# Two weight sums moved to the DMA queues, and two of seven block products with a 512-column operand

## The reference

```python
h = h + 0.5 * swiglu(rms_norm(h, norms[i, 0]), ffn_w_gate[i, 0], ffn_w_up[i, 0], ffn_w_down[i, 0])
...
h = h + 0.5 * swiglu(rms_norm(h, norms[i, 2]), ffn_w_gate[i, 1], ffn_w_up[i, 1], ffn_w_down[i, 1])
```

## Time and profile before

| | |
|---|---|
| median of 3 runs | 1891.37 us (1891.32 to 1891.40) |
| the profiled execution, its own time | 1889.01 us |
| its span, first to last instruction | 1887.2 us |
| TensorE busy | 1858.4 us, 98% |
| VectorE, ScalarE, GpSimd busy | 1354.8, 895.7, 260.9 us |
| stage with the 18 tiles of f = 1 | 521.8 to 703.9 us from the start |
| moved by DMA | 179.88 MB, mean 95 GB/s |

### The profile page before, as it was taken

How to read it: one execution, slowest core, us unless ns; L and a number is a source line. 1 busy time by engine, 2 the same in 40 slices (tenths; PEclk the granted TensorE clock), 3 DMA queues, 4 the chain that set the end, 5 groups by cost and what they waited for, 6 DMA issues and landing times.

```text
span 1887.2 us, 31448 instructions
## 1 busy us (share of the span) xinstructions
PE 1858.4 (98%) x11418; PEld 1615.1 (86%) x11418; DVE 1354.8 (72%) x1983; ACT 895.7 (47%) x1509; POOL 260.9 (14%) x204
## 2 busy tenths in 40 slices
PE   8999999999999999999999999999989999999998
PEld 6899988777799998887899998877658899998886
DVE  8788788774988874357888864269984988874355
ACT  7455542245555563234455553244563655554222
POOL 0000001312100000234000001073243100000225
PEclk9999999999999999999999999999999999999999
DMA  5233333332233333323333332232101233333321
GB/s 180 90 112 101 99 106 105 96 100 86 78 98 95 109 112 111 111 67 101 100 92 99 111 123 96 93 109 68 57 1 46 91 100 99 111 105 118 105 74 56
DMA packets 56753, 179.88 MB, mean 95 GB/s; under 512 B 12144, under 2 KB 12144, under 8 KB 56656
## 3 DMA queue, kind: packets, MB, share of 16 engines
q1 hardware_dynamic: 54656, 173.69, 29.7%
q0 software_dynamic: 928, 3.02, 0.5%
q10 hardware_dynamic: 1088, 2.10, 0.3%
HBM read 175.04 MB, written 3.15 MB: 94 GB/s over the span
## 4 chain that ended last, share of the span: by engine, by line
PE 87%; DVE 9%; ACT 2%; POOL 1%; issue 1%; DMA 0%; DVEq 0%; SPq 0%; POOLq 0%; ACTq 0%
PE ps L2314 36%; PE ps L2276 26%; PE ps L2258 17%; PE ps L2762 2%; PE ps L2425 1%; DVE work L1256 1%; DVE sm L1280 1%; DVE stat L1254 1%; POOL sumsq L1556 1%; DVE x_lo L441 1%; ACT prob L1998 0%; PE ps L2476 0%; PE ps L2288 0%; DVE sm L1299 0%; PE ps L2711 0%
## 5 line engine op out<-in xcount | busy, mean ns | idle before, releaser
L389 DVE TENSOR_TENSOR w_lo<-raw,w_hi 128x1024 fp32r<-128x1024 f32 x174 | 231.6, 1340 | 217.0 <-ACT w_hi L381 216.3
L381 ACT ACTIVATE w_hi<-raw 128x1024 fp32r<-128x1024 f32 x186 | 194.2, 1054 | 293.9 <-PE ps L2276 248.7
L2314 PE MATMUL ps<-xs_hi,w_hi 128*128 128x256 f32 x1088 | 308.2, 283 | 0.5
L2314 PE MATMUL ps<-xs_lo,w_hi 128*128 128x256 f32 x1088 | 307.9, 283 | 0.0
L2314 PE MATMUL ps<-xs_hi,w_lo 128*128 128x256 f32 x1088 | 307.9, 283 | 0.0
L2276 PE MATMUL ps<-act_hi,w_hi 128*128 (+1 forms) x720 | 280.5, 390 | 0.0
L2276 PE MATMUL ps<-act_lo,w_hi 128*128 (+1 forms) x720 | 280.1, 389 | 0.0
L2276 PE MATMUL ps<-act_hi,w_lo 128*128 (+1 forms) x720 | 280.1, 389 | 0.0
L2258 PE MATMUL ps<-x_hi,w_hi 128*128 128x512 f32 x640 | 257.5, 402 | 8.5 <-ACT w_hi L381 7.2
L2258 PE MATMUL ps<-x_hi,w_lo 128*128 128x512 f32 x640 | 250.2, 391 | 0.0
L2258 PE MATMUL ps<-x_lo,w_hi 128*128 128x512 f32 x640 | 249.8, 390 | 0.0
(11 more groups left out here) (412 smaller groups left out, 3545.5 us busy)
## 6 DMA issues: line engine op xcount, KB each, us to landing
raw<-in_weights SPq DMA_DIRECT2D x322, 512.0 KB, 3.6
h<-in_xT ACTq DMA_DIRECT2D x4, 512.0 KB, 6.4
out<-result SPq DMA_DIRECT2D x4, 512.0 KB, 3.0
p_raw<-in_pT POOLq DMA_DIRECT2D x2, 512.0 KB, 4.2
scratch_u<-u_sc SPq DMA_DIRECT2D x1, 512.0 KB, 6.6
u_grp<-scratch_u SPq DMA_DIRECT2D x1, 512.0 KB, 4.1
scratch_y<-y_grp SPq DMA_DIRECT2D x2, 256.0 KB, 3.1
y_ch<-scratch_y SPq DMA_DIRECT2D x1, 512.0 KB, 3.6
```

Source lines behind the costliest of these rows:

```text
L381: act.activation(w_hi[:, slot], raw[:, slot], ACT.Copy).then_inc(hi_ready, 1)
L389: dve.tensor_tensor(w_lo[:, slot], raw[:, slot], w_hi[:, slot].bitcast(F32), SUB)\
L2314: last = pe.matmul(ps[:, bank, 0:HALF], w[:, at, cols], x[:, k], start=(start and k == 0 and part == 0), stop=(stop and k == KH - 1 and pa ...
```

## The change

1. **Sums 1 and 2.** VectorE's 1024-column addition goes. ScalarE's queue loads gate block halves into w_sum[0] and up block halves into w_sum[1], two DMAs of 256 KB; GpSimd waits for them and issues two DMAs that add the left half of the up chunk to both. Odd tiles use a second buffer, `other_sums`, over the first two tiles of act_hi. The loads are issued three tiles ahead (`load_ahead`), at the end of a tile ahead of `silu_right`, after a wait for the last remainder of the tile whose buffer is used again; those of the first two tiles lie in the passage ahead of the first SiLU.
2. **Products B21 and T4.** x_hi and x_lo become the two halves of one tensor, `x_parts`. A product of these two is now, per k-step, one matmul of w_hi by both parts, 512 columns, and one of w_lo by x_hi, 256 columns. The two halves of the bank have to be added afterwards: `gate_left` becomes two additions, and for the right gate half ScalarE copies the bank's right half out, VectorE adds the left half (`gate_right`), and SiLU follows in place.
3. **Order.** In a common tile T2 and T4 are split one by one (512 columns each), T4 first, and the product of gate and up of a tile moves into the next tile, behind its sums. ScalarE's loop ends one turn earlier, as the last tiles load nothing ahead.

```diff
+        x_parts, at_x = sb("x_parts", [P, 2, KD, T], F32R)
+        x_hi, x_lo = x_parts[:, 0], x_parts[:, 1]
...
+        other_sums = over("other_sums", [P, 2, T], at_hi)
...
 def weight_sums(i, b):
-                dve.tensor_tensor(w_sum[:, 0:2], own[:, 0:4:3],
-                                  own[:, 2].unsqueeze(1).to_broadcast([P, 2, T]), ADD)\
-                   .then_inc(fast["w_sums"], 1)
+                dve.wait_ge(added(b), turns_of(f, i, b))
+                dve.tensor_tensor(w_sum[:, 2], loaded_sums(b)[:, 0], own[:, 3], ADD)\
                    .then_inc(fast["w_sums"], 1)
...
 def gate_left(i, b):
+                dve.tensor_tensor(t1[:, b % 2, 0:HALF], left[:, 0:HALF],
+                                  part_sum[:, 0, HALF:], ADD).then_inc(fast["folded"], 1)
+                dve.wait_ge(fast["folded"], counted(1, f, i, b, 1))
+                dve.tensor_tensor(t1[:, b % 2, 0:HALF], left[:, HALF:], t1[:, b % 2, 0:HALF],
+                                  ADD).then_inc(s["gate_scaled"], 1)
+            def gate_right(i, b):
+                dve.wait_ge(fast["half_copied"], counted(1, f, i, b, 1))
+                dve.tensor_tensor(t1[:, b % 2, HALF:], ps[:, banks_of(b)[0], 0:HALF],
+                                  t1[:, b % 2, HALF:], ADD).then_inc(fast["right_scaled"], 1)
...
 def fast_tile(i, b):                                   # VectorE
+                dve.wait_ge(fast["t_ready"], counted(2, f, i, b, 2))
                 weight_sums(i, b + 1)
-                sums_lo(i, b + 1, 0)
+                product(i, b - 1)
+                fourth_lo(i, b + 1)
+                second_lo(i, b + 1)
                 gate_left(i, b)
                 own_lo(i, b + 1, 0)
                 up_right(i, b)
                 sums_lo(i, b + 1, 1)
                 own_lo(i, b + 1, 1)
                 up_left(i, b)
-                product(i, b)
+                gate_right(i, b)
...
+        def block_sums(pool, f, first):                # GpSimd
+            def sums(i, b):
+                pool.wait_ge(loaded(b), turns_of(f, i, b))
+                pool.dma_start(dst[:, 0], up[:, 0:T], accum_op=ADD).then_inc(added(b), 16)
+                pool.dma_start(dst[:, 1], up[:, 0:T], accum_op=ADD).then_inc(added(b), 16)
...
+            def load_blocks(i, b):                     # ScalarE
+                act.dma_start(dst[:, 0], gate[:, 0:T]).then_inc(loaded(b), 16)
+                act.dma_start(dst[:, 1], up[:, T:]).then_inc(loaded(b), 16)
+
+            def load_ahead(i, b):
+                act.wait_ge(fast["t_ready"], counted(2, f, i, b - 2, 2))
+                act.wait_ge(fast["w_sums"], counted(2, f, i, b - 2, 1))
+                load_blocks(i, b)
...
 def silu_right(i, b):
-                act.activation(t1[:, b % 2, HALF:], ps[:, banks_of(b)[0], 0:HALF], ACT.Silu)\
+                act.activation(t1[:, b % 2, HALF:], ps[:, banks_of(b)[0], HALF:], ACT.Copy)\
+                   .then_inc(fast["half_copied"], 1)
+                act.wait_ge(fast["right_scaled"], counted(1, f, i, b, 1))
+                act.activation(t1[:, b % 2, HALF:], t1[:, b % 2, HALF:], ACT.Silu)\
                    .then_inc(s["silu_done"], 1)
...
+            def fast_tile(i, b, ahead=True):           # ScalarE
                 copy_part(i, b, 0)
                 copy_part(i, b, 1)
                 copy_part(i, b, 2)
-                sums_hi(i, b + 1, 0)
+                fourth_hi(i, b + 1)
+                second_hi(i, b + 1)
                 own_hi(i, b + 1, 0)
                 copy_part(i, b, 3)
                 sums_hi(i, b + 1, 1)
                 silu_left(i, b)
                 own_hi(i, b + 1, 1)
+                if ahead:
+                    load_ahead(i, b + 3)
                 silu_right(i, b)
...
+            def paired(bank, at, both, start, stop, done):     # TensorE
+                for k in range(KH):
+                    pe.matmul(ps[:, bank], wf_hi[:, at, k * P:(k + 1) * P], both[:, :, k],
+                              start=(start and k == 0), stop=False, skip_group_check=True)
+                for k in range(KH):
+                    last = pe.matmul(ps[:, bank, 0:HALF], wf_lo[:, at, k * P:(k + 1) * P],
+                                     both[:, 0, k], start=False, stop=(stop and k == KH - 1),
+                                     skip_group_check=True)
+                last.then_inc(done, 1)
...
-                product(left_bank, at["B21"], *unmixed(5), True, True, fast["product"])
+                paired(left_bank, at["B21"], both(5), True, True, fast["product"])
...
-                product(first_bank, at["T4"], *unmixed(6), False, True, chunk_used)
+                paired(first_bank, at["T4"], both(6), False, True, chunk_used)
```

More of the change, by code:

```diff
@@ L1558, in sum_squares @@
                 pool.wait_ge(sum_step, done)
+        def block_sums(pool, f, first):
+            plain = PLAINS[f]
+            pair = plain // 2
+            def sums(i, b):
+                dst = loaded_sums(b)
+                up = A["weights"][bass.ds(i * 4 + (first + 2 * b + 1), 1)]\
+                    .rearrange("a p b f -> (a p) (b f)")
+                pool.wait_ge(loaded(b), turns_of(f, i, b))
+                pool.dma_start(dst[:, 0], up[:, 0:T], accum_op=ADD).then_inc(added(b), 16)
+                pool.dma_start(dst[:, 1], up[:, 0:T], accum_op=ADD).then_inc(added(b), 16)
+            sums(pair, 0)
+            sums(pair, 1)
+            with pool.Fori(pair + 1, NF // 2, 1) as i:
+                sums(i, 0)
+                sums(i, 1)
         def s5_loads(pool):
@@ L1652, in _ @@
             sum_squares(pool, 4)
+            block_sums(pool, 2, STARTS[5])
             sum_squares(pool, 5)
@@ L1728, in gained @@
                        .then_inc(fast["x_gained"], 1)
+            def load_blocks(i, b):
+                gate, up = (A["weights"][bass.ds(i * 4 + (first + 2 * b + k), 1)]
+                            .rearrange("a p b f -> (a p) (b f)") for k in range(2))
+                dst = loaded_sums(b)
+                act.dma_start(dst[:, 0], gate[:, 0:T]).then_inc(loaded(b), 16)
[4 more added lines that the diff above has]
+                load_blocks(i, b)
             def own_hi(i, b, which):
@@ L1784, in opening_tile @@
             def opening_tile():
+                load_ahead(pair, 2)
                 copy_part(pair, 0, 0)
@@ L1794, in opening_tile @@
                 own_hi(pair, 1, 1)
+                load_ahead(pair, 3)
                 silu_right(pair, 0)
-            def fast_tile(i, b):
+            def fast_tile(i, b, ahead=True):
                 copy_part(i, b, 0)
@@ L1841, in passage_of_six @@
                     gained(range(KD))
+                load_blocks(pair, 0)
+                load_blocks(pair, 1)
                 silu(0)
@@ L1897, in ffn_up_act @@
             fast_tile(pair, 1)
-            with act.Fori(pair + 1, NF // 2 - 1, 1) as i:
+            with act.Fori(pair + 1, NF // 2 - 2, 1) as i:
                 fast_tile(i, 0)
                 fast_tile(i, 1)
-            fast_tile(NF // 2 - 1, 0)
+            fast_tile(NF // 2 - 2, 0)
+            fast_tile(NF // 2 - 2, 1, ahead=False)
+            fast_tile(NF // 2 - 1, 0, ahead=False)
             last_tile(NF // 2 - 1, 1)
```

64 lines of the change are left out of this document (51 added, 13 removed).

## The result

The changed kernel takes 1970.58 us (median of 4 runs, 1969.30 to 1975.82) against 1891.38: a ratio of 1.0424, 95% interval 1.0405 to 1.0443. The forecast was 1898.0, with a range that ended at 1914. The loss of 79 us is what the third rival described, at a chance of 0.08.

The account below looks back on a forecast made before the run. The prediction took TensorE's own stream, busy 98% of the span, as the bound. It summed -7.2 + 7.0 + 4.8 + 2.0 = +6.6 us on 1889.0, plus 2.4 for the median: 1898.0 us, range 1886 to 1914.

Parts of the forecast that it names:

- Rival 3: GpSimd's adding DMAs land late: beyond 7.2 us a tile grows by half the excess; at 9 us about 1948; chance 0.08.
- The transfers: Loads and adding DMAs for the sums land at 20.5 us, before VectorE's sum needs them at 21.8: cost 0.
- cover: Time the transfers may slip before a tile suffers, 2.7 us; beyond it half of each microsecond late falls on a tile.
- ScalarE's round: In 44 loop tiles ScalarE's issues and closing copy make product 3 0.16 us late: tiles of 10.13 us, 7.0 us in all.
- X: Delay on ScalarE from the T1/T3 remainder's end to the closing copy, for two DMA issues: 1.17 us; under 1.01 costs nothing.
- Last tiles: Last tile of each stage: two act_high operations ahead of the first copy make product 3 0.49 us late, 2.0 in all.
- Openings: Second tile of each stage: load_ahead waits for the T2/T4 remainder, product 3 is 1.2 us late, four times, 4.8.
- First load_ahead: The load_ahead before the first copy costs nothing: its two issues fit beside ScalarE's work.
- The gain: Products B21 and T4 on TensorE: 544 fewer matmuls at 0.0133 us each, 7.2 us less, a tile of 9.97 us.
- Rival 1: Not slower: ScalarE's round of waits stays under TensorE's, X below 1.01; 1884.2 to 1891.0 us; chance 0.30.
- Rival 2: ScalarE's DMA issue costs 0.487 us: +21.5, 1912.9 us; chance 0.14.
- Rival 4: A wide matmul over two separate halves takes its pair's time: +13.8 us without the 7.2 gain; chance 0.02.

Follow-up runs that it names:

- e4: The changed kernel with GpSimd's second DMAs plain, overwriting instead of adding: 1911.4 us, ratio 1.0107.
- e1: The changed kernel without GpSimd's adding DMAs, VectorE's first sum and ScalarE's T1/T3 split waiting for the plain loads instead: 1905.0 us, ratio 1.0076.
- e5: The changed kernel without GpSimd's adding DMAs and with the loops of ScalarE, VectorE and GpSimd written out, addresses constant: 1891.8 us, ratio 1.0008.
- e7: The changed kernel with four buffers for the sums, loads issued two tiles earlier, and loops of ScalarE, VectorE and GpSimd written out: 1896.0 us, ratio 1.0027.

## Why the prediction was wrong, and where it was right

**The step that failed is "The transfers": cost 0, cover 2.7 us.** It took the load's landing from raw's median, 3.6 us, and the adding DMA's from the latest plain one, 4.5, calling neither a bound. Measured in the chain: 7.09 and 7.35 (medians of the second of each pair: 6.5 and 7.3). By the forecast's own account, from the first issue to the sum, 3.6 + 1.3 + 4.5 = 9.4 us; measured 659.07 - 642.92 = 16.2. The 6.7 us more are 2.7 of cover and 4.0 late, half per tile: 2.0, a tile of 12.0. It is 11.6 in this round (11.4 on the mean), because the part of the ring outside the transfers shrank too: the forecast had 9.2 us from VectorE's sum (offset 1.9) to the issue (11.1), the chain has 642.92 - 635.93 = 7.0. That part contained waits for TensorE, which close up once TensorE is no longer the slowest.

Three facts were wrong in it. The adding was priced as a copy, and it holds the DMA engines 2.15 times as long. Plain, the second DMA of a pair lands after a median of 3.4 us (e4, line 1619), less than the 4.5 of the forecast: what was wrong in that term is the adding. The landings were taken from a kernel in which the engines were 33% busy, and used in one where they are at 65%: in the middle of the stage of f = 1 (600 to 680 us) the median landing of the raw loads themselves went from 3.7 to 6.2 us. Of what the loads were late, most is there without any adding DMA: 5.1 and 5.3 us in e1, against 3.6. And "bytes double, to about two thirds" was right as a mean (0.65) and hid the bursts: raw loads, loads and adding DMAs are all set off by the same tile. In one round of the kernel after, two windows of 2 us each:

```profile
657.00:659.00 2.00, 1.23 (x10) 1.23 (x11) 0.00 (x0) 0.91 (x3) 0.00 (x0) 1.00 1.02 352
...
661.00:663.00 2.00, 2.00 (x19) 2.00 (x19) 1.87 (x5) 2.00 (x5) 0.61 (x1) 1.00 0.03 13
```

Full at 352 GB/s while VectorE waits (DVE 0.00), then 13 GB/s. The Trainium skill, "DMA: Bandwidth & Descriptors", section "Issuing engines are not separate DMA queues", says that the issuing engines share the 16 DMA engines; the trace agrees, raw loads of SyncE's queue land 2.5 us later. The rule stood beside rival 3 and was given 0.08.

**Rival 3** had the right mechanism and the nearest time, 1948 for a landing of 9 us, still 22 us short. Its threshold, 7.2 us, supposed a load that still took 3.6. With both transfers late, 7.35 for the second is more than enough. Its chance was too small: no row priced an adding DMA at all, and an unknown without a row should have been bounded by at least twice its neighbour. Twice 4.5 is the 9 us at which the rival stood.

**ScalarE's round (the forecast itself)** was right as a mechanism and too small. Hidden under the ring in the kernel after, it shows in e1: a tile of 10.30 on the mean instead of 10.13. By steps of the forecast, for the tile of 10.50 us: product 3 to copy 1.74 (forecast 1.64), copy to the end of the T1/T3 remainder 5.64 (5.63), X 1.31 (1.17), copy to gate_right 0.42 (0.41), gate_right to SiLU 0.46 (0.46), SiLU to the next copy 0.49 (0.31), copy to product 3 0.44 (0.51). The mis-sized terms are the turn of ScalarE's loop, 0.18 us of register work between SiLU and copy that the forecast left out (the pieces of line 1985; it comes in every second tile), X, and 0.10 for the first matmul behind a wait. Over the 44 tiles it is 13.9 us (e1 less e5 in the stages), forecast 7.

**Last tiles**: 0.5 each, forecast; the products alone show 10.44 us against 9.99, 0.45. Right. Reordering both ends gave the products alone 4.8 us, where the forecast had 4.8 + 2.0: 1.8 of it in the last tiles, 3.0 in the openings, where the third tile loses 0.18 in return.

**Openings**: 1.2 us each, forecast; in the kernel after, product 3 of the second tile starts at 90.88 against 76.64 + 0.11 + 9.99 + 2.87 = 89.61: 1.27. Right. **First load_ahead**, costed at nothing because it lies beside ScalarE's copy: right in after (0.11 us in the first tile, as before); with the six issues of four buffers it did cost 0.6.

**The gain**: 0.107 a tile forecast, 0.094 measured, so 6.4 us instead of 7.2. The Trainium skill, "TensorE: Matmul & The Clock Gate", section "Back-to-back issue gap", has N/2.4 + 2.5 ns for an isolated matmul; by it a tile would have gained 0.02. The trace disagrees with it here, as the earlier trace rows did.

**Rival 1** (X under 1.01) didn't come in the kernel after, but is what constant addresses make of it (e5). **Rival 2** (issues of 0.487) is out, they take 0.34 to 0.36 in the loops. **Rival 4** is out: a wide matmul takes 0.23 us, not 0.24 and more.

## What to carry to other kernels

A buffer that is used, refilled and used again makes a ring, and it has to be summed with every transfer in it at the landing time that the new traffic will cause, not the old; if it is longer than the tiles it spans, it needs more buffers or shorter landings. Here either one took the ring's waits away: four buffers, with landings that were even later (e7), and plain DMAs with the two buffers (e4). A DMA that adds to its destination isn't a copy: until a run has priced it, take at least twice the engine time. Work moved from an engine with time to spare (VectorE, 31 us of slack a stage) buys nothing; here the half of the change that touched the bound engine gained 4 us alone, once its own small losses at the ends of the stages were taken out.

## What the runs showed of the hardware that was not expected

- An adding DMA of 256 KB occupies the DMA engines 2.15 times as long as a plain one, in 144 packets instead of 80. On quiet engines it runs at 146 to 156 GB/s with a share of 0.94 to 1.06.
- GpSimd's issues of adding DMAs are longer too: a median of 0.86 us for the first of a pair and 1.21 for the second in the kernel after, against 0.54 each for the plain ones of e4. In the round shown the second still begins 0.54 us after the first, so this costs the ring little.
- The first matmul behind a wait takes 0.19 to 0.22 us to the next start instead of 0.12 (613.66 and 613.88 in the kernel without adding DMAs).

What stays open: why the plain loads alone, without adding DMAs, land after 5.1 to 5.3 us (e1) when raw loads of twice the size take 3.5. In the tile shown of e1 a raw load is issued at 609.24, the two loads at 610.70 and 611.22, and the next raw load at 611.30, 1.57 MB in 2.1 us. From 611 to 615 us the DMA engines move 258 to 310 GB/s at a share of 0.89 and 0.81; at that rate the four take 5 to 6 us together (an estimate). That this burst is the reason was not tried by itself.
